# A gated DeltaNet stage: where the gated output of a head is kept, and how its row lengths are summed and averaged

## The reference, cut to what matters

```
o_fwd = delta_rule_chunked(q, k, v, beta[:, :, 0], g[:, :, 0])
o_bwd = flip(delta_rule_chunked(flip(q), flip(k), flip(v), ...))
o = o_fwd + o_bwd
o = o * rsqrt(mean(o * o, axis=-1) + NORM_EPS) * norm_w     # over the 128 columns of a head
o = o * silu(z)
```

## Time and profile before

| | us |
|---|---|
| three runs | 3032.01, 3022.0, 3019.0; median 3022.0 |
| the profiled execution | 3033.88 |
| its span | 3032.2 |
| the DeltaNet stage in it | from about 1240 to 1616 |
| granted PE clock over the span | 0.97 |

### The profile page before, as it was taken

How to read it: one execution, slowest core, us unless ns; L and a number is a source line. 1 busy time by engine, 2 the same in 40 slices (tenths; PEclk the granted TensorE clock), 3 DMA queues, 4 the chain that set the end, 5 groups by cost and what they waited for, 6 DMA issues and landing times. The chain is left out here.

```text
span 3032.2 us, 38463 instructions
## 1 busy us (share of the span) xinstructions
PE 2892.4 (95%) x15223; PEld 2357.6 (78%) x15223; DVE 1282.7 (42%) x1840; ACT 1079.5 (36%) x1845; POOL 1207.0 (40%) x821
## 2 busy tenths in 40 slices
PE   6999999999999989588889999999999999999998
PEld 5878787877888856477767887788888888888887
DVE  5233234322379969666554352322223232232323
ACT  4241313243034548456443122322333323233232
POOL 2222112112122320442322424466666676656663
PEclk9999999999999989788789999999999999999999
DMA  4434232333445366211113536233332333323331
GB/s 115 164 132 137 82 109 90 113 113 110 158 163 171 131 234 227 78 53 43 53 67 129 180 125 208 87 111 97 97 97 91 93 103 117 109 86 97 119 104 56
DMA packets 239570, 352.77 MB, mean 116 GB/s; under 512 B 32928, under 2 KB 186272, under 8 KB 239392
## 3 DMA queue, kind: packets, MB, share of 16 engines
q1 hardware_dynamic: 239392, 350.32, 35.4%
HBM read 263.71 MB, written 96.36 MB: 119 GB/s over the span
## 5 line engine op out<-in xcount | busy, mean ns | idle before, releaser
L102 PE MATMUL pj_acc<-u_hi,pj_w_hi 128*128 128x512 f32 x1464 | 576.6, 394 | 10.6 <-DVE u_lo L823 10.6
L2778 DVE TENSOR_TENSOR x_tm<-m_ps,x_tm 128x512 f32<-128x512 f32 x384 | 264.9, 691 | 745.9 <-PE m_ps L104 745.9
L104 PE MATMUL pj_acc<-u_hi,pj_w_lo 128*128 128x512 f32 x1464 | 571.9, 391 | 0.0
L103 PE MATMUL pj_acc<-u_lo,pj_w_hi 128*128 128x512 f32 x1464 | 571.6, 390 | 0.0
L551 POOL TENSOR_TENSOR pj_w_lo<-pj_w_raw,pj_w_hi 128x1024 fp32r<-128x1024 f32 x61 | 158.7, 2602 | 722.3 <-ACT pj_w_hi L600 722.3
L2660 POOL TENSOR_TENSOR m_lo<-gate,held 128x1024 fp32r<-128x1024 f32 x96 | 237.5, 2498 | 270.0 <-ACT held L2577 270.0
L102 PEld LDWEIGHTS pj_acc<-u_hi,pj_w_hi 128*128 128x128 f32 x1464 | 275.9, 188 | 85.7 <-issue 18.2
L104 PEld LDWEIGHTS pj_acc<-u_hi,pj_w_lo 128*128 128x128 f32 x1464 | 276.1, 189 | 58.1
L103 PEld LDWEIGHTS pj_acc<-u_lo,pj_w_hi 128*128 128x128 f32 x1464 | 276.2, 189 | 56.4
L102 PE MATMUL m_ps<-held 128*128 128x512 f32 x768 | 299.5, 390 | 2.4 <-DVEq L2759 2.4
L102 PE MATMUL m_ps<-held,m_h_hi 128*128 128x512 f32 x768 | 299.5, 390 | 0.0
(11 more groups left out here) (316 smaller groups left out, 4934.7 us busy)
## 6 DMA issues: line engine op xcount, KB each, us to landing
gate<-in_w_mlp_dram SPq DMA_DIRECT2D x48, 1024.0 KB, 5.4
gate<-in_w_mlp_dram SPq DMA_DIRECT2D x96, 512.0 KB, 3.7
proj<-pj_stage SPq DMA_DIRECT2D x61, 768.0 KB, 3.5
pj_w_raw<-in_w_in_dram SPq DMA_DIRECT2D x61, 512.0 KB, 5.2
gate<-proj SPq DMA_DIRECT2D x24, 768.0 KB, 4.3
mo_w_raw<-in_w_out_dram SPq DMA_DIRECT2D x48, 256.0 KB, 2.8
rpb_bias<-pj_shut SPq DMA_DIRECT2D x48, 192.0 KB, 3.0
rpb_bias<-rpb_near SPq DMA_DIRECT2D x24, 384.0 KB
```

The costliest lines, as they stand in the source:

```text
L102: pe.matmul(out, w_hi, x_hi, start=first, stop=False)
L103: pe.matmul(out, w_hi, x_lo, start=False, stop=False)
L104: return pe.matmul(out, w_lo, x_hi, start=False, stop=last)
L2778: dve.tensor_tensor(xt, ps2[:, q % 4], xt, ALU.add).then_inc(added, 1)
```

## The change

Four edits, all in `deltanet`:

1. `out_norm` writes into `work` and no longer into `oc[0]`; `out_gate` works in `work`, and the store reads `work`. ACT's wait for the store is gone from the end of the solve and stands now in step 4 of the scan, ahead of the tanh that overwrites `work`. In its old place, ahead of the first output copy of step 0, ACT now waits until DVE has read `oc[0]` (`onorm`).
2. `out_gate` moves from round 15 to behind round 17.
3. `out_lengths` multiplies the squares by all 128 columns of `ones`. Its 4 products of 128x128 fill the whole bank `ps[:, 3]`, so a third waits until the mean of the one before is read out. The thirds move from rounds 3, 4, 5 to 3, 5, 7.
4. The mean is taken in three parts in rounds 4, 6, 8; the root moves from 8 to 9, the diagonal from 8 to 10, the spreads to 11, 13, 15 and the norms to 12, 14, 16.

```diff
-SUM_AT, SQUARES_AT, LENGTHS_AT, MEAN_AT, ROOT_AT, DIAG_AT = 0, 2, (3, 4, 5), 6, 8, 8
-SPREAD_AT, NORM_AT, GATE_AT = (10, 12, 14), (11, 13, 15), 15
+SUM_AT, SQUARES_AT, LENGTHS_AT, MEAN_AT, ROOT_AT, DIAG_AT = 0, 2, (3, 5, 7), (4, 6, 8), 9, 10
+SPREAD_AT, NORM_AT = (11, 13, 15), (12, 14, 16)
...
                 sp.wait_ge(S["out_done"], i + 1)
-                sp.dma_start(flat(o_t[dsl(i + HEADS)].rearrange("a p n -> p a n")), oc[0]).then_inc(S["stored"], 16)
+                sp.dma_start(flat(o_t[dsl(i + HEADS)].rearrange("a p n -> p a n")), work[:]).then_inc(S["stored"], 16)
...
-                act.wait_ge(S["stored"], i * 16 + 16)
                 if more:
                     for n in STRICT_LAST:
                         strict_decays(i + 1, n)
...
+                    if step == 0:
+                        act.wait_ge(S["onorm"], NTB * i)
                     for j, d, t in live_chains(step):
...
                         act.wait_ge(S["z_in"], i * 16 + 16)
-                        act.wait_ge(S["onorm"], NTB * i)
+                        act.wait_ge(S["stored"], i * 16 + 16)
                         act.activation(work[:], zt, ACT.Tanh, scale=0.5).then_inc(S["zt"], 1)
...
                 pe.wait_ge(S["osq"], h + 1)
-                for t in range(4 * tb, 4 * tb + 4):
-                    last = pe.matmul(ps[:, 3, 0, t:t + 1], th[:, t * P:(t + 1) * P], ones[:, 0:1], start=True, stop=True)
+                if tb:
+                    pe.wait_ge(S["omean"], NTB * h + tb)
+                for j in range(4):
+                    t = 4 * tb + j
+                    last = pe.matmul(ps[:, 3, j], th[:, t * P:(t + 1) * P], ones[:], start=True, stop=True)
                 last.then_inc(S["oss"], 1)
...
-            def out_mean(h):
-                dve.wait_ge(S["oss"], NTB * h + NTB)
-                dve.tensor_scalar(oms[:], ps[:, 3, 0, 0:NT], 1.0 / P, EPS, ALU.mult, ALU.add).then_inc(S["omean"], 1)
-                dve.wait_ge(S["omean"], h + 1)
+            def out_mean(h, tb):
+                dve.wait_ge(S["oss"], NTB * h + tb + 1)
+                dve.tensor_scalar(oms[:, 4 * tb:4 * tb + 4], ps[:, 3, :, 0], 1.0 / P, EPS, ALU.mult, ALU.add).then_inc(S["omean"], 1)
+                if tb + 1 < NTB:
+                    return
+                dve.wait_ge(S["omean"], NTB * h + NTB)
                 dve.reciprocal(orr[:], oms[:]).then_inc(S["orr"], 1)
...
-                dve.scalar_tensor_tensor(three(oc[0])[:, tb], three(oc[0])[:, tb], nw[:], flat(ps[:, 3]),
+                dve.scalar_tensor_tensor(three(work[:])[:, tb], three(oc[0])[:, tb], nw[:], flat(ps[:, 3]),
...
-                dve.scalar_tensor_tensor(oc[0], oc[0], 0.5, zt, ALU.mult, ALU.mult).then_inc(S["out_done"], 1)
+                dve.scalar_tensor_tensor(work[:], work[:], 0.5, zt, ALU.mult, ALU.mult).then_inc(S["out_done"], 1)
...
-                        if k == GATE_AT:
-                            out_gate(i - 1)
                 dve.sem_inc(S["s0"], 1)
+                if i:
+                    out_gate(i - 1)
```

More of the change, by code:

```diff
@@ L1979, in main @@
                             out_sum(i - 1)
-                        if k == MEAN_AT:
-                            out_mean(i - 1)
+                        if k in MEAN_AT:
+                            out_mean(i - 1, MEAN_AT.index(k))
                         if k == DIAG_AT:
```

## The result

The changed kernel takes 3010.4 us (median of 7 runs, 3007.8 to 3012.4) against 3022.6 before (7 runs, 3019.0 to 3033.5). The ratio is 0.9941, 95% interval 0.9924 to 0.9958. The profiled execution took 3012.1, 21.8 less than the profiled one of before. The forecast was 3001 for the median and 24 less for the profiled execution. The change is clear of noise, but 12 us is less than the 15 that the prediction asked for in a "faster".

What follows compares the result with a forecast made beforehand. The DeltaNet stage was taken as bound by a PE, ACT, PE, DVE chain, losing time to store waits and low clock. Solves 14 plus ends 10 made 24 us less, median 3001; range 2984 to 3017.

Steps and rivals of the forecast that it cites:

- its own case: Whole kernel: 3001 us, from 2990 to 3008, with most low clock in the solves gone; chance 0.55.
- the clock stays low: Rival for the solves: 128 columns come too seldom, solves keep 130.9 us but for the gate; 12 us less, 3010; chance 0.28.
- The lengths cost the same with 128 columns.: Length products in the solves: 128 columns cost about what one column does; 0 taken, at most 3 us in all.
- The columns hold the clock in their rounds.: Solves, rounds 3, 5 and 7: 128-column products do real work where the clock fell, so most low time goes.
- The argument from head 0: Head 0's solve does the same without the one-column products and stays at clock 1.00 throughout.
- The root.: ACT's root in round 9, directly ahead of the exponentials, delays PE's step 12: +3.4 us in heads 1 and 2.
- The low time that stays, "about one such stretch of 3.4 us a head at half price".: Low clock left in the three solves: 4.3 us given back from 18.4 less, leaving 14 us.
- the rival that makes it slower: Rival: the root's 3.4 us hole drops the clock in round 10 and it stays down; 3043 us; chance 0.05.
- The full-clock sum.: Solves of heads 1, 2, 3 at full clock: 38.3, 38.3 and 35.9, together 112.5 us against 130.9.
- The gate: Output gate on DVE, 1.76 us, moved behind round 17 beside the Gram products: costs 0 in heads 1 and 2.
- The ends, 10 us.: Solve end to first state copy, without the store's wait: 2.9 + 2.9 + 4.5 us less in heads 1, 2, 3.
- From the execution to the median.: Profiled execution 3033.9 - 24 = 3010; median 12 us lower before, so 3007 or 2998 after; 3001 taken.

Runs made afterwards that it cites:

- a_onecol: The changed kernel with its length products back at one column, same rounds and waits: 3015.8 us, ratio 0.9959 to the kernel before.
- home_only: The kernel before with edits 1 and 2 alone (output in `work`, store's wait moved, gate behind round 17): 3004.5 us, ratio 0.9928.
- home_c42: The kernel before with edits 1 and 2, and length products of 42 columns in their old rounds: 3003.8 us, ratio 0.9920.
- b_again: The kernel before, unchanged, profiled a second time on another occasion: 3028.3 us, ratio 1.0009.
- a_exp_late: The changed kernel with the next head's exponentials moved from rounds 9 and 12 to 11 and 13: 3002.4 us, ratio 0.9918 to the kernel before.
- after_again: The changed kernel, unchanged, run a second time: 3010.0 us, ratio 0.9944 to the kernel before.
- home_again: The kernel before with edits 1 and 2 alone, run once more: 3002.7 us, ratio 0.9916.
- c42_exp: The kernel before with edits 1 and 2, 42-column lengths in old rounds, exponentials moved to rounds 11 and 13: 2991.6 us, ratio 0.9887.
- c42_exp_again: c42_exp, unchanged, on another occasion: 2997.2 us, ratio 0.9918 to the kernel before.

## Why the prediction was right, and where it was not

The time lies in the range (2984 to 3017) and the direction was forecast; the median is 9 us above the forecast and 2 above the stretch of its own case (2990 to 3008). The chance of 0.63 was on a time under 3007, which did not come. The number alone can't tell the forecast's case from its first rival: for *the clock stays low* the prediction had 3010, which is the measured time. The traces tell them apart: that rival wants the solves at 125 or more with the low time as it was, and they took 119.9 with 27 us in place of 64.5. By its steps:

- *The lengths cost the same with 128 columns.* Right: 1.06 us for a third against 1.05 at the full clock.
- *The columns hold the clock in their rounds.* Right as to the outcome: 0 of 15 heads stayed low in rounds 3 to 8. As to the cause, it is only in part shown: with one column in the same rounds (a_onecol) 2 of 3 heads kept the clock there as well, and the new spacing did some of it. The argument from head 0 was weak. Head 0 lacks not only the one-column products but also the sum and its hole in PE, and 6 of 9 heads with one column, the new home and the old rounds kept the full clock in rounds 3 to 8. The stretch from 1449.4 to 1452.8 also holds 64x64 products, which the prediction left out.
- *The root.* Right in mechanism: in round 10 of heads 1 and 2 PE waits for the copy behind table load, root, table load and exponentials. Of the 3.4 us, 2.76 were a hole. The chain is shorter than the sum had it because the table load did not wait for the mean and reciprocal: it started at 1362.92, DVE's mean at 1363.59 and its reciprocal at 1363.78, and the root followed at 1364.22. Nor is the hole new with round 9: home_only and home_c42, with the root in round 8, have one of 2.51 in the same place, and so does head 2 of b_again, 2.41, which had the full clock there. Head 3 has no such hole, but one of 1.0 ahead of the first spread.
- *The low time that stays, "about one such stretch of 3.4 us a head at half price".* This is the term that was mis-sized. 27 us stayed in the three heads in one execution and 26 in the other, not 10, of them 26 and 21 in rounds 8 to 17, behind the root's hole and the waits for diagonal and norm. The solves took 119.9 and not 112.5 + 4.3 = 116.8. a_exp_late, in which the hole of the root is gone, came to 113.7 and 7.7 us less in time; so this one placement cost the change about as much as the median missed. I had seen the hole and the falling clock as the rival that makes it slower; it came at a small part of that price. The turns alone don't bring it: head 3 of a_exp_late has them in the same rounds and stood at 0.99.
- *The full-clock sum.* Head 3 of a_exp_late, at 0.99, took 35.8 us, against 35.9 in the sum. The wait of a third for a mean, put at 0 and at worst 0.5, was 0.6 in each head; there was also a wait of 1.39 for a norm ahead of the last spread.
- *The gate.* Right: home_only's head 3 loses it from its solve, with 1.2 us from round 15 to 16 against 3.0 before, and its 1.74 us beside the Gram products held nobody.
- *The ends, 10 us.* Too much for both: 6.7 in one execution and 8.1 in the other. 2.9 + 2.9 + 3.1 is what comes where an end runs at the full clock: heads 1 and 3 here began their end at the low clock (6.1 and 3.4 in place of 4.9 and 1.9), heads 1 and 3 of after_again did not (4.4 and 2.1).
- *The moved waits cost nothing.* Right: neither the tanh nor the output copies of step 0 waited.
- *From the execution to the median.* 24 us were forecast for the profiled execution and 21.8 came. Part of that is luck: solves and ends, from which the 24 were added up, gave 17.7, and the rest came from the scans and from scatter of the clock behind the stage. But then 9 of the 12 us that lie between an execution and the median of before were given the median of after as well (3010 and 3001). Both profiled executions of before are among its longer runs (3033.9 and 3033.3; the runs reach from 3011 to 3038), those of after lie within 2 us of their median. The runs of after scatter less (3008 to 3016), and with that the distance is gone. Whether the quicker runs of before differ by low clock in the solves was not seen, since none was profiled.

What the change gives, in parts: home and gate alone brought ratios of 0.9928 and 0.9916, about 22 to 25 us; the lengths, means and later rounds on top took back some 4 to 8 (0.9941, 0.9944), though their intervals overlap. They bring clock in rounds 3 to 8 and pay for it with three more waits, for a mean, the diagonal and a norm (0.6, 1.0 and 1.4 us). The price shows in head 3 near the full clock: 35.8 us (a_exp_late) against 33.2 and 33.3 (home_again, home_only), 2.6 a head. Home and gate do more than their own waits, too: 5.4 us of gate and 7 at the ends make 12 of the 22 to 25, and the rest goes with less low clock (42 us in home_only's solves, 20 in home_again's, 65 and 70 in the two of before); why was not tested. The lowest medians are those of c42_exp, where the thirds need no wait and the root stands apart from the exponentials: 2991.6 and 2997.2 us. Its first ratio, 0.9887, is below both kernels; its second, 0.9918, is that of home_again (0.9916) and a_exp_late (0.9918), and its interval overlaps that of the change.

## What to carry to other kernels

When an edit fills one engine to hold its clock, ask what else it moves: here the wide products were free and their rounds kept the clock, but the waits and later rounds that came with them cost 2.6 us a head at the full clock, and the full clock laid bare a hole behind the root of 2.5 to 2.8 us. A chain that is covered by a slow stretch (a root between two table loads, a wait for a store) shows only when the stretch gets quicker, so sum the new schedule at the full clock and look for its longest hole. And take the scatter of a kernel seriously: one profiled execution of before had 6 us more in a solve than the other with the same instructions, so compare several before giving an edit the difference.

## What the runs showed of the hardware

- The granted clock can stay at 0.50 while PE is busy without a break: 18.0 us of 18.0 in c42_exp_again, in turns, 32x32 and 64x64 products and lengths of 42 columns. With 12 products of 128 columns in rounds 3, 5 and 7 it never stayed down in rounds 3 to 8, over 15 heads (at most 1.4 us).
- For the clock the same instructions have two outcomes. Rounds 3 to 8 of the six executions with the new home and the old rounds took 9.5 or 16.6 us and nothing between, in 14 and 4 heads. The four had a hole of 2.8 to 2.9 us at the sum, the others 1.0 to 2.4, and the length of the hole went with where the clock stood when the solve began. Which of the two is the cause, and what sets the phase, was not found.
- A product of 128 partitions with a fresh set of 128x128 weights costs the same with 1 or 128 columns: 1.05 and 1.06 us for eight records.
